# Fixed PSUM banks for the memory steps, norms of the first token tiles further ahead, and two small re-orderings in a hybrid conv/mLSTM layer

## The reference

```
mod = silu(c) @ w_ada + b_ada                      # shift, scale, gate, twice
h = rmsnorm(x, g_mix) * (1 + sc1) + sh1
xin, bg, cg, q, k, v, o, ig, fg, gate_c, gate_m = split(h @ w_in + b_in)
p_conv = (bg * conv3(cg * xin)) @ w_proj_conv
hm = mlstm_chunkwise(q, k, v, ig, fg)              # chunks of 128 tokens, 4 heads, state C (128 x 256) and n
p_mlstm = (sigmoid(o) * rmsnorm(hm, g_head)) @ w_proj_mlstm
x = x + gt1 * ((sigmoid(gate_c) * p_conv + sigmoid(gate_m) * p_mlstm) @ w_out)
h = rmsnorm(x, g_ffn) * (1 + sc2) + sh2
x = x + gt2 * ((silu(conv3(h @ w_up_a)) * (h @ w_up_g)) @ w_down)
y = rmsnorm(x, g_final)
```

## Time and profile before

| | |
|---|---|
| runs | 1375.95 us median (1372.84 to 1376.09) |
| profiled execution | 1372.99 us; span of its slowest core (4) 1371.7 us |
| spans of the eight cores | 1362.9 to 1371.7 us |
| TensorE busy | 1263.1 us (92%) |
| VectorE busy | 697.5 us (51%) |
| ScalarE busy | 529.2 us (39%) |

### The profile page before, as it was taken

How to read it: one execution, slowest core, us unless ns; L and a number is a source line. 1 busy time by engine, 2 the same in 40 slices (tenths; PEclk the granted TensorE clock), 3 DMA queues, 4 the chain that set the end, 5 groups by cost and what they waited for, 6 DMA issues and landing times.

```text
span 1371.7 us, 21457 instructions; the slowest of 8 cores (1362.9 to 1371.7 us)
## 1 busy us (share of the span) xinstructions
PE 1263.1 (92%) x7662; PEld 690.8 (50%) x7662; DVE 697.5 (51%) x1268; ACT 529.2 (39%) x1013; POOL 76.5 (6%) x149
## 2 busy tenths in 40 slices
PE   0677999997899999999998999989999999999998
PEld 0354455665656665666654444444444444444443
DVE  0574332576843346555654423378732365556534
ACT  2464122654522225544433331465522245544202
POOL 1000000000000000000000000000000000100000
PEclk9997999999999999999999999999999999999999
DMA  9988024267493646343252782505346074441503
GB/s 174 233 194 136 1 39 75 50 107 124 85 189 60 106 91 131 69 81 63 46 111 85 175 154 54 101 1 93 84 101 112 13 152 93 74 81 32 108 0 123
DMA packets 35128, 130.38 MB, mean 95 GB/s; under 512 B 2764, under 2 KB 3020, under 8 KB 35024
## 3 DMA queue, kind: packets, MB, share of 16 engines
q0 software_dynamic: 24944, 93.74, 40.6%
q1 hardware_dynamic: 10080, 35.27, 7.8%
HBM read 214.34 MB, written 8.39 MB: 162 GB/s over the span
## 4 chain that ended last, share of the span: by engine, by line
PE 83%; DVE 6%; DMA 4%; ACT 3%; issue 3%; POOL 0%; DVEq 0%; ACTq 0%; SPq 0%; POOLq 0%
PE psum L508 54%; PE psum L1258 11%; PE psum L1113 4%; PE psum L793 4%; DMA wslot<-w_in 3%; PE psum L1348 2%; PE psum L691 2%; PE psum L484 1%; DVE C L869 1%; DVE arena L841 1%; ACT arena L860 1%; PE psum L867 1%; DMA arena<-bada_row 1%; ACT sqj L433 1%; PE psum L418 1%
## 5 line engine op out<-in xcount | busy, mean ns | idle before, releaser
L508 PE MATMUL psum<-arena,wslot 128*128 128x512 bf16 (+1 forms) x4640 | 830.7, 339 | 11.6 <-DVE arena L915 3.8
L508 PEld LDWEIGHTS psum<-arena,wslot 128*128 128x128 bf16 x4640 | 452.5, 98 | 372.0 <-issue 31.6
L1187 DVE SCALAR_TENSOR_TENSOR arena<-arena,pcol_t 128x1028 f32<-128x1028 f32 (+1 forms) x88 | 113.3, 1287 | 92.8 <-ACT arena L1184 88.2
L1258 PE MATMUL psum<-wslot,arena 128*128 128x512 bf16 x704 | 153.2, 380 | 1.5 <-ACT arena L488 1.5
L1258 PEld LDWEIGHTS psum<-wslot,arena 128*128 128x128 bf16 x704 | 68.8, 98 | 84.2 <-issue 2.2
L1069 ACT ACTIVATE arena<-psum,pcol_t 128x512 bf16<-128x512 f32 (+1 forms) x80 | 47.9, 603 | 162.2 <-PE psum L508 161.1
L433 ACT ACTIVATE sqj<-arena 128x1024 bf16<-128x1024 f32 (+1 forms) x49 | 51.6, 1054 | 137.6 <-DVE arena L1261 96.0
L1189 ACT ACTIVATE arena<-arena 128x1028 f32<-128x1028 f32 (+1 forms) x44 | 46.6, 1059 | 121.1 <-DVE arena L1187 121.1
L1073 DVE TENSOR_TENSOR arena<-psum,arena 128x512 f32<-128x512 f32 (+1 forms) x40 | 23.3, 585 | 73.4 <-PE psum L508 72.5
L1113 PE MATMUL psum<-wslot,arena 128*128 128x512 bf16 (+1 forms) x272 | 60.3, 379 | 0.2 <-DVE arena L492 0.2
L793 PE MATMUL psum<-wslot,arena 128*128 128x512 bf16 (+1 forms) x272 | 59.2, 379 | 0.0
(11 more groups left out here) (176 smaller groups left out, 1084.8 us busy)
## 6 DMA issues: line engine op xcount, KB each, us to landing
wslot<-w_in POOLq DMA_DIRECT2D x32, 1024.0 KB, 12.2
arena<-xin SPq DMA_DIRECT2D x32, 512.0 KB, 16.1
wslot<-w_ada POOLq DMA_DIRECT2D x12, 1024.0 KB, 13.3
wslot<-w_up_a POOLq DMA_DIRECT2D x10, 1024.0 KB, 10.1
wslot<-w_up_g POOLq DMA_DIRECT2D x10, 1024.0 KB, 11.8
wslot<-w_down POOLq DMA_DIRECT2D x8, 1024.0 KB, 9.0
y<-arena SPq DMA_DIRECT2D x16, 512.0 KB, 2.7
xt<-xin SPq DMA_DIRECT2D x15, 512.0 KB, 5.2
```

What stands on the lines that cost most here:

```text
L508: S.op("pe", lambda e: e.matmul(psum[:, b, 0:n], lhsT=wv[:, k, wcol0:wcol0 + 128], rhs=src[:, k, t0:t0 + n], start=(k == 0), stop=(k == 7) ...
L1187: S.op("dve", lambda e: e.scalar_tensor_tensor(out=t3[:, T0:NT], in0=a_s[:, s_ + T0:s_ + NT], scalar=pcol[:, cw + s_:cw + s_ + 1], in1=t3[ ...
L1258: S.op("pe", lambda e: e.matmul(psum[:, b, :], lhsT=act_t[jj][:, t0:t0 + 128], rhs=wv[:, jj % 8, :], start=(jj == 0), stop=(jj == NFF - 1) ...
```

## The change

There are five parts.

1. SyncE waits for the K weight (the fifth weight tile) and not for the third before it asks for x tile 4 and those after it.
2. One counter pair (`norm_upto(na, nb)`) drives the norms of prefix and first front: the ScalarE part of tiles up to na, the VectorE part up to nb. It runs ahead of `kproj(c)` by 5 tiles at the start and by up to 13 at the end, so that all but the last of the nine front tiles are normalised before the first front. Four more buffers (`xfr`) hold them.
3. Two of the four K projections of stage 0 move ahead of the prefix sums, between the last steps of `gates_prefix`.
4. Memory steps: `at_K`, `at_A` and `at_D` no longer take banks 0 to 3 but fixed ones: K bank 6, A bank 7, D banks 4 and 5. K is emptied by four ScalarE operations in place of one of VectorE. The steps are put at new places and partly cut in halves.
5. In `during_down` the load of a tile is written one job earlier.

```diff
+        xfr = [at("E", 8192 + i * 2048, [128, D], BF16) for i in range(4)]
...
+        def norm_upto(na, nb):
+
+            while XN["a"] < na or XN["b"] < nb:
+                if XN["b"] < nb and XN["b"] < XN["a"]:
+                    next(XN["gen"].pop(XN["b"]), None)
+                    XN["b"] += 1
+                else:
+                    g_ = x_tile(XN["a"])
+                    next(g_)
+                    XN["gen"][XN["a"]] = g_
+                    XN["a"] += 1
...
-            k_, v_ = r_wslot[W["slot_of"][2]].w
+            k_, v_ = r_wslot[W["slot_of"][4]].w
             S._wait("sp", {k_: v_})
...
-        for g in range(4):
-            for i in range(4):
-                if g < 3:
-                    xprefix(g * 4 + 4 + i)
-                elif i < 3:
-                    front_norm(i)
-                if g < 3 and i == 3:
-                    tgroup(g + 1)
-                kproj(g * 4 + i)
-            if g == 1:
+        for c in range(NPF):
+            ahead = (0, 1, 1, 1, 1, 2, 2, 3, 3, 4, 4, 5, 5, 6, 7, 8)[c]
+            norm_upto(min(c + 5 + ahead, NPF + 8), min(c + 5 + ahead // 2, NPF + 8))
+            if c in (3, 7, 11):
+                tgroup(c // 4 + 1)
+            kproj(c)
+            if c == 7:
...
             def at_K(c):
-                b = next_bank()
+                b = XB + 2
...
-                S.op("dve", lambda e: e.tensor_tensor(out=ktok[0:p, c, :]..., in0=psum[0:p, b, :]..., in1=wG..., op=ALU.mult), ...)
+                for h in range(4):
+                    S.op("act", lambda e: e.activation(out=ktok[0:p, c, h * 128:(h + 1) * 128], in_=psum[0:p, b, h * 128:(h + 1) * 128], func=AF.Identity,
+                                                       scale=wG[0:p, c * 4 + h:c * 4 + h + 1]), reads=[r_bank[b], r_gout], writes=[r_ktok[c]])
             def at_A(c):
-                b = next_bank()
+                b = XB + 3
...
-            def at_D(c):
-                for half in range(2):
-                    b = next_bank()
+            def at_D(c, halves):
+                for half in halves:
+                    b = XB + half
...
-            parts = [(-0.7, at_K), (-0.7, at_A), (0.2, at_X), (0.3, at_new), (0.3, at_den), (0.45, lambda c: at_sq(c, lo)), (0.55, lambda c: at_sq(c, hi)),
-                     (0.65, at_f), (0.75, lambda c: at_hm(c, lo)), (0.85, lambda c: at_hm(c, hi)), (1.45, at_D)]
-            per = nblk / (nch + 0.6)
-            todo = [((c + f) * per, i, fn, c) for c in range(nch) for i, (f, fn) in enumerate(parts)]
-            todo += [((c + 0.5) * per, 99, at_old, c + 1) for c in range(-1, nch - 1)]
+            parts = [(-0.42, at_K), (-0.52, at_A), (0.05, at_X), (0.22, lambda c: at_new(c, lo)), (0.22, at_den), (0.3, lambda c: at_new(c, hi)),
+                     (0.35, lambda c: at_sq(c, lo)), (0.45, lambda c: at_sq(c, hi)), (0.6, at_f), (0.7, lambda c: at_hm(c, lo)), (0.8, lambda c: at_hm(c, hi)),
+                     (1.45, lambda c: at_D(c, (0,))), (1.53, lambda c: at_D(c, (1,)))]
+            per = nblk / (nch + 0.65)
+            todo = [((c + 0.2 + f) * per, i, fn, c) for c in range(nch) for i, (f, fn) in enumerate(parts)]
+            todo += [((c + 0.2 + f) * per, 99, lambda c, hh=hh: at_old(c, hh), c + 1) for c in range(-1, nch - 1) for f, hh in ((0.4, lo), (0.5, hi))]
...
         for g in range(3):
-            if g == 0:
-                front_norm(3)
             transp(tiles, hT, LAY[0][0][g * 3][0], r_h0[g], G1, r_G1, SH1)
-            for f in range(g * 3 + 4, min(g * 3 + 7, 9)):
-                front_norm(f)
+            if g == 1:
+                norm_upto(NPF + 9, NPF + 9)
...
-        interleave(gates_prefix(NPF), [(lambda h=h: proj(si_q, h * 128, hT, rd_h, tbs0, evq(h))) for h in range(4)])
+        interleave(gates_prefix(NPF), [(lambda h=h: proj(si_q, h * 128, hT, rd_h, tbs0, evq(h))) for h in range(4)]
+                   + [(lambda h=h: proj(si_k, h * 128, hT, rd_h, tbs0, evk(h))) for h in range(2)])
```

52 lines of the change are left out of this document (28 added, 24 removed).

## The result

In the same rounds the kernel before took 1373.8 us and the changed one 1362.4 us (medians of seven and of five executions; executions in which the clock of one die had fallen are left out here and in the table below). The ratio is 0.9915 [0.9902, 0.9929]: 0.85% faster, some 11 us. The forecast was 1346 us with 1363 as its upper end; the profiled execution took 1363.9. So the sign was right, and a good three fifths of the gain did not come.

A forecast was written before the change was run, and what follows sets the result against it. TensorE was taken as the bound, so only gaps and slow-clock stretches could be given back. Terms 3 + 6 + 2.5 + 2.4 + 9 + 6 = 28.9 us off 1373.0 gave 1344.1, plus 2 for the median: 1346; range 1330 to 1363.

The forecast's parts named there:

- SyncE's wait: Start: holding x tiles back lands the K weight 5 us sooner, of which 3 us stay; bounds 0 and 5.
- The first lands 2 us after 45.4: Start: the first held-back x tile lands about 2 us after the K weight, the fifth at 55.4 us.
- Norms ahead: First front: tiles normed early cut first transposition to first Q projection from 18.6 to 12.7 us; 6 gained, bounds 3 and 8.
- so I count nothing gained: Prefix: ScalarE needs 12.0 us against 11 a group, so nothing gained on the other 5.2 us of gaps.
- the start gives nothing back: Rival: x tiles late by what the weight is early, ScalarE overfull, front late; 1353, up to 1356 us; chance 0.08.
- Clock: First Q projection and prefix matmuls run nearer 2.4 GHz with fewer gaps; 2.5 of 4.5 us gained, bounds 0 and 4.5.
- K projections in the gap: Before the prefix sums: two K projections cover VectorE's chain in a 4.5 us gap; 2.4 us gained, bounds 0 and 2.5.
- Stage 0's steps: Stage 0's memory steps: 16 us gaps and 5 clock removed, 12 added by A's waits and clock; 9 gained, bounds 0 and 18.
- Stage 1's steps: Stage 1's memory steps: 6.9 us copy waits go, 2 from gaps and clock, 3 lost; 6 gained, bounds 0 and 10.
- a whole block of 1.7 us now stands between, more than the copy's 1.02 and its start: Stage 1's memory steps: one block covers ScalarE's copy of X, removing new's 6.9 us of waits for it.
- Second front: Second front: nothing gained; loads already start when buffers free, and TensorE's 3.96 us wait on a VectorE scaling stays.
- the memory steps gain nothing: Rival: A on bank 7 and K on bank 6 put back what free banks give; 1361 us, chance 0.17.

The follow-up runs named there:

- e10: e9 with SyncE's wait back at the third weight tile; time the same as e9's within 0.4 us, 1.1 on the mean end.
- e2: Changed kernel with the first front's norms run late, in the last four K blocks; prefix 48.5 us, time not distinguishable from the changed kernel's.
- e9: Changed kernel with e5's start and, in stage 1 alone, e6's earlier places; 1351.3 us, 11.1 under the changed kernel.
- e5: Changed kernel with front squares issued behind the fourth transposition and the ninth tile's square ahead of the front; 7.6 us less by medians, 5.4 by ratios.
- e3: Changed kernel with the memory steps of before (banks, places, K emptied on VectorE); 8 us more, 9 by the ratios.
- e4: Changed kernel with K's bank emptied by one VectorE multiplication instead of four ScalarE pieces; 4 us more.
- e6: Changed kernel with squares, f and head scalings at earlier places in the memory steps; 4.0 us less by medians, 1.9 by ratios.

## Why the prediction was wrong, and where it was right

Term by term, on the mean of the cores unless said otherwise:

- **SyncE's wait (3 us forecast, nothing measured).** The first half was right: the K projection starts at 45.5, as forecast. The x tiles then land at 52.1 (first square) to 59.8 us on core 2, and the second transposition starts its main part at 60.95 and not at 57. "The first lands 2 us after 45.4" was the wrong step: the first took over 6. (The 45.4 takes 6.4 us a weight tile, where the working above it gives 6.2; that is 0.4 us.) The rule that the prediction quoted against this part from the Trainium skill (DMA: Bandwidth & Descriptors, Issuing engines are not separate DMA queues) had it right, and the trace agrees: e10 moves the wait by two weight tiles and the time is unchanged within 0.4 us.
- **Norms ahead (6 forecast).** The front gave its 6.1 us. The failed step is the sentence on the prefix, "so I count nothing gained": it costed ScalarE's work as an amount, 12.0 us against 11 a group, and took the excess as nothing. The prefix became 10.4 us longer. Five to six of them are x tiles that are late against a K projection that is early, by e2 and by e9 with e10; the start of K gives these back. The others are the order: squares whose tiles had not landed stand ahead of an emptying for which TensorE waits. e5 shows it: the same squares, behind the emptying, 6.6 us less prefix. The rival "the start gives nothing back" described this (0.08), and priced it at 7 to 10 us; wait and norms together gave 0.8 of the 9 us forecast, 8 short, and 10 with the clock's part.
- **Clock (2.5).** 1.0: the prefix sums took 31.7 and not 32.7 us. The first Q projection still took 5.36 us on core 2, at a granted clock of 0.64, with 3.78 us of waiting in the front just ahead of it.
- **K projections in the gap (2.4).** 2.8, right (3.8 us up to the V projections, 1.0 of them the clock).
- **Stage 0's steps (9).** 8.7, less 0.9 ahead of them: right in size, and e3 gives 8.2 for undoing it. The parts come near: A's waits on the state addition are 6.9 us in six on core 2 (10 forecast), K on ScalarE helps (e4). The wait for the last row was left in at 3.29; on the slowest core it is 9.0. The prediction's estimate from the Trainium skill (VectorE: DVE Perf Modes, The TRN2 errata) was 0.25 us for a ScalarE piece of K. The trace shows more, 1.14 us for four (923.49 us on core 2), 0.285 each, and the measurement decides; the sum does not change.
- **Stage 1's steps (6).** Minus 2.0: the largest miss with the start. The failed step is "a whole block of 1.7 us now stands between, more than the copy's 1.02 and its start". It took the copy as ready to start when X ends. In the new order X follows f of the previous chunk by two blocks in three chunks, the copy stands behind the head scalings, these wait for f, and f stands behind the burst. e6 undoes exactly this: 4.4 us, and 109.9 is 2.4 under before. Against before the copy's waits grew by 1.1 us (8.0 for 6.9) and A's two on the state addition (2.0, forecast 3) came new, while 2.2 us of waits of blocks and scores went. How much of the 2.0 us is the steps and how much the banks stays open, since e3 is 2.4 over with the old steps. One of the prediction's own signs of being wrong came with this: the part takes as long as before (114.3 us, before 112.3).
- **Second front (0).** Right: TensorE's wait there is 3.97 us, as in the earlier trace rows.
- **From the mean to the slowest core.** The mean end gained 11.9 us; the profiled spans of the slowest cores 9.1, as core 2 waited 9.0 us for the row, where the mean of the cores is 4.6. This belongs to that execution: in the five of the changed kernel the slowest core is 2, 7, 5, 3 and 3, and the medians gained 11.4. So it explains half a microsecond of the miss. What makes the row later on one core than on another was not tried.

Sum on the mean: 0.8 (start) + 3.8 + 7.8 (stage 0) - 2.0 (stage 1) are 10.4 of the 11.9; 0.4 lost in the merge, and 1.9 gained in pieces of 0.2 to 1.0 us up to stage 1 that no term had. The 17 us short of the forecast are then 8 in the start, 8 in stage 1 and 1.5 of clock, with 1 more in stage 0 and some small gains against it.

The measured time is also that of the first rival, "the memory steps gain nothing" (1361). That is luck: stage 0's steps gained what was forecast for them, and the time came from losses at the start and in stage 1.

## What to carry to other kernels

An engine's queue is costed by who stands behind whom, not by its sum of work: an operation that may have to wait for a transfer belongs behind the emptying for which TensorE waits, even if its result could be used earlier (e5). When a short operation is moved away from the one that waited on it, follow the queue of its engine back to the first thing that is itself waiting; here the 1 us copy hung on a 3.5 us burst of another engine (e6). And where a wait does not move the time when taken away, look for a second one at the same place before calling it free: the bank and the weight tile behind stage 0 gave nothing each alone; with the other mends, the two together took nearly all of both waits away.
